# The output product of a retention branch, regrouped: four passes over one head each, against two passes over two heads each

## What is computed

```
def _retention_branch(zb, s0, pos):
    ...
    y = y * lax.rsqrt(jnp.mean(y * y, axis=-1, keepdims=True) + NORM_EPS)
    out = jax.nn.silu(g) * y.reshape(bsz, t, B_V_WIDTH)
    return out, s_new
...
    merged = (gates[:, :, 0] * (y_a.astype(h.dtype) @ p['w_branch_a'])
              + gates[:, :, 1] * (y_b.astype(h.dtype) @ p['w_branch_b']))
    out = merged.astype(h.dtype) @ p['w_out']
```

## Time and profile before

| | |
|---|---|
| median of 3 executions | 4783.89 us (4774.67 to 4784.2) |
| the profiled execution, its own time | 4781.01 us |
| its span (first to last instruction) | 4779.2 us |
| TensorE matmuls busy | 4349.6 us, 91% of the span |
| VectorE busy | 1968.0 us, 41% |
| ScalarE busy | 1398.4 us, 29% |
| granted TensorE clock, mean | 0.962 of 2.4 GHz |

### The profile page before, as it was taken

One profiled execution on the slowest core, in us unless ns is written; L12 is line 12 of the kernel. 1 busy time (PEld: TensorE's weight loads), 2 busy tenths in 40 slices (PEclk: granted clock), 3 DMA queues, 4 the chain that ended last, 5 costly groups with the idle time before them and its releaser, 6 DMA issues.

```text
span 4779.2 us, 87090 instructions
## 1 busy us (share of the span) xinstructions
PE 4349.6 (91%) x37724; PEld 3751.5 (78%) x37724; DVE 1968.0 (41%) x2998; ACT 1398.4 (29%) x2131; POOL 239.7 (5%) x399
## 2 busy tenths in 40 slices
PE   6799999999978887999878999999999788879997
PEld 1598988888965566999817888988888656669996
DVE  0444434443234544444405344444442354444443
ACT  1333333333222222222204333333332222232222
POOL 0000000000011110000000000000000111100000
PEclk9999999999989998999988999999999899989998
DMA  7212212211245542222261112211222455512221
GB/s 248 79 55 62 62 57 64 65 61 58 70 135 200 186 158 68 67 75 73 60 243 46 58 58 62 62 60 60 62 65 75 160 186 176 168 30 73 77 74 60
DMA packets 482309, 448.88 MB, mean 94 GB/s; under 512 B 17894, under 2 KB 399728, under 8 KB 481024
## 3 DMA queue, kind: packets, MB, share of 16 engines
q1 hardware_dynamic: 434352, 294.99, 19.9%
q0 software_dynamic: 30192, 115.10, 7.3%
q10 hardware_dynamic: 17408, 33.56, 1.9%
HBM read 345.82 MB, written 97.76 MB: 93 GB/s over the span
## 4 chain that ended last, share of the span: by engine, by line
PE 83%; DVE 7%; DMA 5%; ACT 2%; issue 2%; POOL 0%; SPq 0%; DVEq 0%; ACTq 0%
PE ps L672 81%; DVE scr L1739 2%; DMA scr<-in_ada_w_dram 2%; PE ps L676 2%; DMA scr<-scratch_z 1%; ACT scr L1259 1%; DMA w_raw<-in_w_branch_a_dram 1%; DVE scr L1741 1%; DVE scr L1811 1%; ACT w_hi L1272 1%; DVE acc L1739 1%; DVE lw L1739 1%; DVE h_lo L1739 0%; DVE w_lo L1752 0%; DMA w_raw<-in_w_in_dram 0%
## 5 line engine op out<-in xcount | busy, mean ns | idle before, releaser
L672 PE MATMUL ps<-h_hi,w_hi 128*128 128x320 f32 x4544 | 1104.4, 324 | 119.6 <-DVEq L1747 74.9
L672 PE MATMUL ps<-scr 64*64 64x64 f32 (+10 forms) x14016 | 1048.5, 259 | 65.7 <-DMA scr<-in_ada_w_dram 54.5
L672 PE MATMUL ps<-h_lo,w_hi 128*128 128x320 f32 x4544 | 1042.6, 311 | 0.0
L672 PE MATMUL ps<-h_hi,w_lo 128*128 128x320 f32 x4544 | 1041.2, 310 | 0.0
L672 PEld LDWEIGHTS ps<-scr 64*64 64x64 f32 (+5 forms) x14016 | 670.5, 141 | 416.1 <-issue 372.7
L672 PEld LDWEIGHTS ps<-h_hi,w_hi 128*128 128x128 f32 x4544 | 749.5, 190 | 194.4 <-issue 148.5
L672 PEld LDWEIGHTS ps<-h_lo,w_hi 128*128 128x128 f32 x4544 | 767.3, 190 | 0.0
L672 PEld LDWEIGHTS ps<-h_hi,w_lo 128*128 128x128 f32 x4544 | 766.2, 189 | 0.0
L1259 ACT ACTIVATE scr<-ps 128x512 f32<-128x512 f32 (+8 forms) x702 | 345.2, 492 | 1060.7 <-PE ps L672 816.7
L1272 ACT ACTIVATE w_hi<-w_raw 128x1024 fp32r<-128x1024 f32 (+1 forms) x468 | 410.8, 878 | 820.7 <-PE ps L672 616.3
L1752 DVE TENSOR_TENSOR w_lo<-w_raw,w_hi 128x1024 fp32r<-128x1024 f32 (+1 forms) x468 | 469.6, 1003 | 357.2 <-ACT w_hi L1272 336.8
(11 more groups left out here) (143 smaller groups left out, 2982.8 us busy)
## 6 DMA issues: line engine op xcount, KB each, us to landing
w_raw<-in_w_in_dram SPq DMA_DIRECT2D x180, 512.0 KB, 3.7
scr<-in_ada_w_dram SPq DMA_DIRECT2D x24, 2048.0 KB, 7.8
scratch_z<-scr SPq DMA_DIRECT2D x128, 320.0 KB, 2.2
scr<-in_state_ret_dram POOLq DMA_DIRECT2D x64, 512.0 KB, 4.8
out_dram<-scr ACTq DMA_DIRECT2D x64, 512.0 KB, 2.9
w_raw<-in_w_ffn_up_dram SPq DMA_DIRECT2D x64, 512.0 KB, 4.0
w_raw<-in_w_ffn_down_dram SPq DMA_DIRECT2D x128, 256.0 KB, 2.7
scr<-scratch_z POOLq DMA_DIRECT2D x24, 1280.0 KB, 8.0
```

What stands on the lines that cost most here:

```text
L672: return pe.matmul(out, lhsT, rhs, start=start, stop=stop, skip_group_check=True)
```

## The change

There are two products in the place of four, each over two heads with eight contraction tiles. `bb0` (heads 0 and 1) runs beside head 2, with two units at each place. `bb1` (heads 2 and 3) runs behind head 3 by itself. Beside heads 1 and 3 there is nothing. Head 1's result goes to the upper four tiles of `h`, head 2's to `r`, head 3's to the lower four tiles of `h`. The stand-alone product takes its first two tiles together, two contraction tiles at a time, and waits by name for head 2's mark, then for head 3's.

```diff
-    for h in range(RH):
-        jobs.append((f"bb{h}", 8, 4, "v"))
+    for f in range(RH // 2):
+        jobs.append((f"bb{f}", 8, 8, "v"))
...
-        bb_v = io["w_branch_b"].rearrange("l (f k p) (c n) -> l f c p k n", p=128, k=4, n=128)
+        bb_v = io["w_branch_b"].rearrange("l (f k p) (c n) -> l f c p k n", p=128, k=8, n=128)
...
+        def split_rows(h):
+
+            return R if h == 2 else H, 4 * (h == 1)
...
-            return f"bb{h - 1}" if h else "ba"
+            return {0: "ba", 2: "bb0"}.get(h)
...
-                in_r = k < 4 if name == "ba" else int(name[2:]) % 2 if name[:2] == "bb" else name[:2] == "do"
-                return (R if in_r else H)[part][:, k]
+                in_r = k < 4 if name in ("ba", "bb1") else name[:2] == "do"
+                return (R if in_r else H)[part][:, k - 4 if name == "bb1" and k >= 4 else k]
...
-                point = units_of(l, beside_head(h), 1 if h else 2)
+                point = units_of(l, beside_head(h), 2)
...
-                gemm(l, f"bb{RH - 1}", [(RH * l + RH - 1, "lo4")] * 2)
+                gemm(l, "bb1", [(RH * l + h, "lo4") for h in (2, 2, 3, 3)])
...
-                    ac.wait_ge(mm_done, START[l, f"bb{h - 1}"])
+                    ac.wait_ge(mm_done, START[l, "bb1" if h == 3 else "bb0"])
```

More of the change, by code:

```diff
@@ L456, in part_of @@
         def part_of(l, name, emit, each=1):
-            tiles_, units = units_in(name)
+            tiles_, units = units_in(name) if name else (0, 0)
             at_ = [0]
@@ L644, in _ @@
                 for t in range(KD):
-                    po.wait_ge(psum_read_v, freed(START[l, f"bb{RH - 1}"] + t, "v"))
+                    po.wait_ge(psum_read_v, freed(START[l, "bb1"] + t, "v"))
                     po.dma_start(MS[:, t], scratch["m"][:, t]).then_inc(m_in, 16)
@@ L767, in units_of @@
             def units_of(l, name, each=1):
-                g0, units = START[l, name], units_in(name)[1]
+                g0, units = (START[l, name], units_in(name)[1]) if name else (0, 0)
                 def unit(i, q):
@@ L1537, in retention @@
                 M = lambda name: done("ac_rt", n, name)
-                point = high_parts_of(l, beside_head(h), 1 if h else 2)
-                Y = R if h % 2 else H
+                point = high_parts_of(l, beside_head(h), 2)
+                Y, y0 = split_rows(h)
                 def bank(u):
@@ L1570, in high @@
                     W("ve_rt", f"m{b}")
-                    do(Y[0][:, 0:4, block_of(b)], VY[:, :, block_of(b)])
+                    do(Y[0][:, y0:y0 + 4, block_of(b)], VY[:, :, block_of(b)])
                     M(f"hi{b}")
@@ L1701, in _ @@
                     retention(l, h)
-                gemm(l, f"bb{RH - 1}")
+                gemm(l, "bb1")
                 for j in range(4):
@@ L2123, in retention @@
                 M = lambda name: done("ve_rt", n, name)
-                point = sums_of(l, beside_head(h), 1 if h else 2)
+                point = sums_of(l, beside_head(h), 2)
                 turning = rope(l, h + 1) if h < RH - 1 else iter(())
-                Y = R if h % 2 else H
+                Y, y0 = split_rows(h)
                 g16 = float((1.0 - 2.0 ** (-5.0 - h)) ** DEC_T)
@@ L2164, in low @@
                     W("ac_rt", f"hi{b}")
-                    tt(Y[1][:, 0:4, block_of(b)], VY[:, :, block_of(b)], Y[0][:, 0:4, block_of(b)].bitcast(F32), SUB)
+                    tt(Y[1][:, y0:y0 + 4, block_of(b)], VY[:, :, block_of(b)], Y[0][:, y0:y0 + 4, block_of(b)].bitcast(F32), SUB)
                     M(f"lo{b}")
```

## The result

The changed kernel takes 4837.32 us (median of 4, 4835.44 to 4841.16) against 4783.07 us for the kernel before: a ratio of 1.0118, 95% interval 1.0104 to 1.0132. It is slower by 54 us, where 42 was forecast.

A forecast was written before the change was run, and what follows sets the result against it. TensorE's stream was taken as the bound, so gaps decide. Per layer, heads 1, 2, 3 and the end: -15.5 +21.8 -15.0 +29.6 = +20.9 us; two layers +41.8 on 4781.0 give 4823 us, range 4798 to 4850.

The forecast's parts named there:

- head 3: Head without cover in each layer: gives back 17.0 us by its stretches, 15.0 after the clock charge.
- Head 1: Head without cover in each layer: gives back 17.1 us by its stretches, 15.5 after the clock charge.
- B: First to sixth state step of heads 1 and 3: 25.3 us without cover, gives back 9.9.
- C: Sixth state step to second gated product: 4.8 us in head 1 (gives back -0.7), 3.1 in head 3 (1.0).
- what the clock cost: Gaps before the last steps of uncovered heads: one lower-clock loss each, 1.6 us in head 1, 2.0 in head 3.
- D: Second gated product to the head's end: gives back 2.2 us in head 1, 0.4 in head 3.
- A: Values' arrival to first state step, heads 1 and 3: 11.4 us falls to about 5.7, paced by ScalarE's evictions.
- first rival: Heads 1 and 3: the clock falls for good and they give back nothing; 4884 us, chance 0.08.
- Head 2: Head with double cover: +1.8 before the transposes, +19.5 where TensorE leads, +0.5 for wider splits; +21.8 us a layer.
- The end: Stand-alone product: +28.3 for 96 more pairs, +0.5 second-tile split, +0.8 third-tile wait; +29.6 us a layer.
- the faster case: TensorE's own work alone bounds heads 1 and 3, which give back 27.0 and 25.2 us; 4772 us, chance 0.05.
- that rival's 4836 us: Transposes leave the clock low: first step and first scores at 1.2 GHz, 3.3 us in each of four heads; chance 0.05.

The follow-up runs named there:

- the kernel with two mends: The changed kernel with the fifth state piece's store early and the stand-alone product's second-tile split ahead of head 3: 4813.46 us, ratio 1.0061 to the kernel before.

## Why the prediction was right, and where its terms were off

**The bound.** TensorE's stream, dense under cover, was the right reading. Unread matmuls in place of the cover bring the heads back to within 1 to 3 us of their length, and each half of the change alone has its places' lengths. The way and the size came out, 54 us against 42, and most of the difference is head 3: 4.7 of 8.3 us in the first layer, 4.9 of 7.7 in the second.

**Head 1.** That it came within 1.4 us (14.1 for 15.5) is partly luck: B gave back 4.3 us less than forecast, C gave 1.7 more, and what the clock cost, charged with 1.6 by itself, lies within the measured B and D.

**A, the transposes.** 5.7 us were forecast to remain. Head 1 has 6.0 (1502.76 to 1508.74) and head 3 has 5.9. The reason that was given, ScalarE's evictions, isn't shown: TensorE has transposes in work for 6.05 us in head 1 without a wait, and for 5.5 of the 5.9 us in head 3.

**B, first to sixth step.** 25.3 us were forecast, 9.9 given back. Head 1 took 29.6 and head 3 28.7. This is the first term that was off. "The fifth step comes some 1 us before its piece" took the two times of the round trip, 3.2 and 4.5 us, from covered heads, where the stores lie far apart. Without cover the second store goes out while the load before it runs, and its own took 3.6 us in head 3 and 5.1 in head 1. The fifth step waited 2.25 and 2.45 us, and the clock fell in the wait, another 1.3 to 1.5 us in the third product. (In the second layer head 3's waited 1.72 us, and the third product stayed at 2.84.) Without the stores B is 24.7 us.

**C.** 4.8 us in head 1 and 3.1 in head 3 were forecast; it was 3.1 in both. The next head's queries didn't hold up the sixth piece.

**D.** In head 1 2.2 us were forecast to come back from VectorE; 1.7 did, though the eighth step and the product behind it ran at the lower clock. In head 3, "without cover waits for the eighth state piece: gives back 0.4" is the step that failed most. The wait was named, and its size was wrong. Without stores D takes 19.0 us, so the 22.1 us that the forecast left leave room for 3 us of wait and what follows from it; the prediction doesn't say how it came by that. It was 7.4 us: the stretch grew from 22.5 to 26.5, with a wait of 6 us and a slow eighth step behind it. The store of the fifth piece stands behind two roots in ScalarE's stream, and moving that one store gives 7 us back.

**The clock.** 1.6 and 2.0 us a head were charged. The mean fell to 0.80 and 0.86, and the trace has the falls just where TensorE waits, as forecast. Filling the waits is worth about 3 us in head 3. In head 1 the scatter of 3.6 us hides it. The prediction's own sign for its first rival, a clock below 0.8 over a whole head, was badly set: head 1 of the changed kernel has 0.80, and head 1 of the kernel with two mends 0.77 and 0.78, yet these kernels take 4837 and 4813 us, far from the 4884 us of that rival.

**Head 2.** +21.8 forecast, +22.8 and +19.8 (85.6 before, 105.4 after) in the two layers. Against the five records of 84.9 to 85.6 it is +20, so the forecast was 2 us too high, and the first layer's short record of head 2 hides that.

**The end.** +29.6 forecast, +30.8 in the first layer and +32.3 in the second. The wait for the split was right, and so was the third tile's wait:

```profile
1765.14 0.55 PE L676 MATMUL ps<-r_hi,w_hi 128*128 128x320 f32 x2 [0.80 <-DVE w_lo L1756]
```

That is 0.80 us, where 0.79 was read off the product `out`. The rest in the first layer is a slower start, eleven pairs at 0.53 us. What the prediction underrated is what the missed overlap is worth: at most 3 us, it said, and 5.5 to 6.6 were measured, since the start at the lower clock goes too and the first wait for `lo4` disappears behind 7 us of work.

**The rivals.** The clock didn't stay low, and the faster case didn't come. The transposes didn't leave the clock low either, although that rival's 4836 us are nearer to the measured 4837 than the forecast is; that is chance. In head 1 of the changed kernel they stand alone after 14 us of idle time, as they did not before. The rows give, for 4 us each, TensorE busy, its matmuls, the granted clock, the DMA share and GB/s:

```profile
1504.00:1508.00 4.00, 4.00 (x23) 0.55 0.09 32
1508.00:1512.00 4.00, 4.00 (x22) 1.00 0.00 0
```

Only transposes run before 1508.74, and the first step behind them took the full-clock 1.70 us. By the rule of the Trainium skill (TensorE: Matmul & The Clock Gate, "Part 4: PE-mode transpose") they would not have counted. The measurement decides against it here.

## What to carry to other kernels

Filler work beside a chain of dependent steps is worth what it hides, and that is read per place. Here a head full already took 28.3 us more for 20 to 23, and a head left bare gave back only 10 to 14 of the 28.3 that were taken out. One reason is that its own round trips (a buffer's store, then its next load) come to light: with one store moved, head 3 gave back 17. Before taking cover away, list for every ring of buffers when its store could be issued and when it is; a store that stands behind two waiting instructions cost nothing under cover, where the load behind it landed just in time, and 7 us without. And when a piece of work is announced as early by a list of waits, look for the last instruction in the other engines' streams that it also needs.

## What the runs showed of the hardware that was not expected

The same head, with the same instructions, took 74.3 to 77.9 us, depending on how long it waited for its fourth and fifth pieces (1.5 to 3.1 us together) and which of its short products met TensorE's lower clock. The third product took 2.84 to 4.54 us, the one behind the eighth step 3.7 to 6.1, the last 3.60 to 5.3. And from the issue of a store of 512 KB to the issue of the load that waits for it, it was 3.1 us (head 3) and 4.2 us (head 1) in the changed kernel when the store ran alone, and 4.0 and 5.4 us beside one load of the same size.
